# The first output tile of five large matrix products runs k-tile by k-tile beside other TensorE work, and the last square no longer passes through GpSimd

## The reference, cut to what matters

```
for li in range(2):
    g = norm_g[li]
    xn = rmsnorm(h, g[0])
    mix = mix_even(xn) if li == 0 else mix_odd(xn)       # RWKV-7 + mLSTM, or retention
    h = h + rmsnorm(mix, g[1])
    f = square(relu(rmsnorm(h, g[2]) @ ffn_up[li])) @ ffn_down[li]
    h = h + rmsnorm(f, g[3])
    h = h + sigmoid(h @ ple_gate[li]) * (p[li] @ ple_proj[li])
```

## Time and profile before

| | |
|---|---|
| median of 3 runs | 2152.05 us (2147.31 to 2153.11) |
| the profiled execution | 2154.12 us, of which the span of instructions is 2152.3 us |
| granted TensorE clock, mean | 0.942 |
| PE busy | 92% of the span |
| DVE / ACT / POOL busy | 46% / 31% / 3% |

### The profile page before, as it was taken

How to read it: one execution, slowest core, us unless ns; L and a number is a source line. 1 busy time by engine, 2 the same in 40 slices (tenths; PEclk the granted TensorE clock), 3 DMA queues, 4 the chain that set the end, 5 groups by cost and what they waited for, 6 DMA issues and landing times.

```text
span 2152.3 us, 39908 instructions
## 1 busy us (share of the span) xinstructions
PE 1975.4 (92%) x16899; PEld 1805.8 (84%) x16899; DVE 998.9 (46%) x1493; ACT 672.8 (31%) x928; POOL 72.3 (3%) x82
## 2 busy tenths in 40 slices
PE   8988887888587999999899999999999799999989
PEld 7967775777265999999899976666999699999978
DVE  6546762555514442342266745555642643234244
ACT  4222214323113332332243123335432433233222
POOL 0000000111000000000100000000001000000000
PEclk9998985889678999999999999999999899999999
DMA  5202110000221222222313224444223122222221
GB/s 197 96 30 79 40 64 0 3 2 3 101 81 48 78 89 97 88 88 97 108 49 118 88 90 177 179 171 186 99 90 96 40 97 88 89 97 88 89 97 60
DMA packets 44750, 187.01 MB, mean 87 GB/s; under 512 B 5480, under 2 KB 5992, under 8 KB 39272
## 3 DMA queue, kind: packets, MB, share of 16 engines
q1 hardware_dynamic: 44648, 185.53, 25.1%
HBM read 160.48 MB, written 25.03 MB: 86 GB/s over the span
## 4 chain that ended last, share of the span: by engine, by line
PE 84%; DVE 10%; ACT 3%; issue 2%; POOL 0%; DMA 0%; DVEq 0%; POOLq 0%; SPq 0%; ACTq 0%
PE ps L2136 52%; PE ps L2019 7%; PE ps L332 3%; PE ps L727 2%; PE ps L1681 2%; PE ps L2084 1%; DVE h_a L1909 1%; PE ps L2094 1%; PE ps L2078 1%; DVE free L414 1%; PE ps L1705 1%; PE ps L350 1%; PE ps L1667 1%; PE ps L2074 1%; DVE rb L369 1%
## 5 line engine op out<-in xcount | busy, mean ns | idle before, releaser
L2124 DVE TENSOR_TENSOR w_low<-slot,w_high 128x1024 fp32r<-128x1024 f32 x240 | 293.5, 1224 | 495.0 <-ACT w_high L2120 494.9
L2120 ACT ACTIVATE w_high<-slot 128x1024 fp32r<-128x1024 f32 x240 | 254.0, 1059 | 797.6 <-PE ps L2136 709.5
L2136 PE MATMUL ps<-x_high,w_high 128*128 128x260 f32 x1600 | 323.3, 283 | 1.1 <-issue 1.1
L2136 PE MATMUL ps<-x_high,w_low 128*128 128x260 f32 x1600 | 322.9, 283 | 0.0
L2136 PE MATMUL ps<-x_low,w_high 128*128 128x260 f32 x1600 | 322.4, 283 | 0.0
L2136 PE MATMUL ps<-hidden_high,w_low 128*128 128x260 f32 x1536 | 309.5, 283 | 0.0
L2136 PE MATMUL ps<-hidden_high,w_high 128*128 128x260 f32 x1536 | 309.4, 283 | 0.0
L2136 PE MATMUL ps<-hidden_low,w_high 128*128 128x260 f32 x1536 | 309.0, 283 | 0.0
L2136 PEld LDWEIGHTS ps<-x_high,w_high 128*128 128x128 f32 x1600 | 247.7, 189 | 1.8 <-issue 1.5
L2136 PEld LDWEIGHTS ps<-x_high,w_low 128*128 128x128 f32 x1600 | 247.2, 189 | 0.0
L2136 PEld LDWEIGHTS ps<-x_low,w_high 128*128 128x128 f32 x1600 | 246.6, 189 | 0.0
(11 more groups left out here) (555 smaller groups left out, 2634.4 us busy)
## 6 DMA issues: line engine op xcount, KB each, us to landing
slot<-in_w SPq DMA_DIRECT2D x240, 512.0 KB, 3.8
h_a<-in_rst SPq DMA_DIRECT2D x16, 1024.0 KB, 4.9
out_rst_o<-h_a SPq DMA_DIRECT2D x16, 1024.0 KB, 3.9
slot<-in_w SPq DMA_DIRECT2D x2, 2048.0 KB, 8.4
h_a<-in_x SPq DMA_DIRECT2D x4, 520.0 KB, 5.2
h_a<-in_x SPq DMA_DIRECT2D x1, 2080.0 KB, 7.6
out_y<-h_a SPq DMA_DIRECT2D x8, 260.0 KB
con<-in_con SPq DMA_DIRECT2D x1, 2062.0 KB, 16.0
```

Source lines behind the costliest of these rows:

```text
L2120: nc.scalar.activation(wh[c % 2], raw[c % 4], ACT.Copy).then_inc(s_wh, 1)
L2124: nc.vector.tensor_tensor(wl[c % 2], raw[c % 4], wh[c % 2].bitcast(F32), ALU.subtract).then_inc(s_wl, 1)
L2136: mm = pe.matmul(ps[:, 2 * par + hf, 0:HALF], w[c % 2][:, at], y(kt, hf), start=(start and kt == 0 and w is wh and y is x), stop=(stop and ...
```

## The change

1. `pe_prenorm` takes a function `beside`. After the norm product of k-tile kt it runs the 6 matmuls of k-tile kt-1 of the next product's first output tile (`first_tile`), and the last one after the loop. The first of them waits for the PSUM pair, for `w_low` of chunk 0, and each for its `x_low`. This is done at `in0`, `up0a` and `up1a`.
2. At the start, ACT makes `w_high` of chunk 0 ahead of k-tile 5, and DVE makes its `w_low` behind `x_low` 5; chunk 1 stays last.
3. In `pe_proj` the gate's first tile goes in beside the embedding products: k-tiles 0 to 3 behind products 4 to 7, then k-tiles 4 to 7. ACT copies products 0 and 1 out before its first `hh` copy, and from there product mt+2 behind `hh` mt.
4. `pe_postnorm` multiplies twice: `ss`, now the sum of only 7 squares, and then the eighth square itself (`sqr[1]`), added in PSUM. POOL makes one addition fewer per norm.
5. The loops over output tiles begin with the second group of four; tiles 1 to 3 stand in front of the loop as code of their own.

```diff
-        def pe_prenorm(pe, n):
+        def pe_prenorm(pe, n, beside=None):
             for kt in range(KD):
                 pe.wait_ge(s_xg, 8 * n + kt + 1)
                 for hf in range(2):
                     mm = pe.matmul(ps[:, 4 + hf, 0:HALF], C("mean_d"),
                                    hid[:, 24 + kt, hf * HALF:(hf + 1) * HALF], start=(kt == 0), stop=(kt == KD - 1))
-            mm.then_inc(s_st, 1)
+                if kt == KD - 1:
+                    mm.then_inc(s_st, 1)
+                if beside and kt:
+                    beside(kt - 1)
+            if beside:
+                beside(KD - 1)
 
         def pe_postnorm(pe, n):
-            pe.wait_ge(s_ss, 8 * n + 8)
-            for hf in range(2):
-                mm = pe.matmul(ps[:, 4 + hf, 0:HALF], C("mean_d"), ss[:, hf * HALF:(hf + 1) * HALF],
-                               start=True, stop=True)
+            for first, sums, w in [(True, ss, (s_ss, 7 * n + 7)), (False, sqr[1], (s_sq, 8 * n + 8))]:
+                pe.wait_ge(*w)
+                for hf in range(2):
+                    mm = pe.matmul(ps[:, 4 + hf, 0:HALF], C("mean_d"), sums[:, hf * HALF:(hf + 1) * HALF],
+                                   start=first, stop=not first)
             mm.then_inc(s_st, 1)
...
-        def act_prenorm(act, n, h, gain, ready, xg):
+        def act_prenorm(act, n, h, gain, ready, xg, ahead=None):
             for kt in range(KD):
+                if kt == 5 and ahead:
+                    ahead()
                 act.wait_ge(*ready(kt))
...
         def pool_sum(pool, n):
-            for mt in range(KD):
+            for mt in range(KD - 1):
                 pool.wait_ge(s_sq, 8 * n + mt + 1)
...
+        def first_tile(pe, t0, base, waits, x=part_of(xh), lo=part_of(xl)):
+
+            def beside(kt):
+                if kt == 0:
+                    pe.wait_ge(s_bank, t0 + 1)
+                    pe.wait_ge(s_wl, base + 1)
+                for w in waits(kt):
+                    pe.wait_ge(*w)
+                mm = pe_step(pe, 0, 0, x, lo, kt, True, True)
+                if kt == KD - 1:
+                    mm.then_inc(s_tile, 1)
+            return beside
...
+            gate_tile = first_tile(pe, GEMMS[f"gate{lyr}"][1], CHUNKS[f"gate{lyr}"],
+                                   lambda kt: [(s_gl, 8 * lyr + kt + 1)], part_of(hh, 8), part_of(hl))
             for mt in range(KD):
                 if mt >= 2:
                     pe.wait_ge(s_pjc, 8 * lyr + mt - 1)
...
                 mm.then_inc(s_pj, 1)
+                if mt >= 4:
+                    gate_tile(mt - 4)
+            for kt in range(4, KD):
+                gate_tile(kt)
 
         def act_ple(act, lyr, hn, more):
             a = nc.scalar
-            for mt in range(KD):
-                act.wait_ge(s_h, 8 * (2 * lyr + 1) + mt + 1)
-                a.activation(hh[:, 8 + mt, :], hb[lyr][:, mt, :], ACT.Copy).then_inc(s_gh, 1)
-                act.wait_ge(s_pj, 8 * lyr + mt + 1)
-                p4 = 4 + 2 * (mt % 2)
-                a.activation(two(hid[:, mt, :]), ps[:, p4:p4 + 2, 0:HALF], ACT.Copy).then_inc(s_pjc, 1)
+            for mt in range(-2, KD):
+                if mt >= 0:
+                    act.wait_ge(s_h, 8 * (2 * lyr + 1) + mt + 1)
+                    a.activation(hh[:, 8 + mt, :], hb[lyr][:, mt, :], ACT.Copy).then_inc(s_gh, 1)
+                if mt + 2 < KD:
+                    act.wait_ge(s_pj, 8 * lyr + mt + 3)
+                    p4 = 4 + 2 * (mt % 2)
+                    a.activation(two(hid[:, mt + 2, :]), ps[:, p4:p4 + 2, 0:HALF], ACT.Copy).then_inc(s_pjc, 1)
...
             pe.wait_ge(s_first, 32)
-            pe_prenorm(pe, 0)
-            pe_split(pe, "in0", lambda kt: [(s_xl, kt + 1)], only=NB)
+            pe_prenorm(pe, 0, first_tile(pe, GEMMS["in0"][1], CHUNKS["in0"], lambda kt: [(s_xl, kt + 1)]))
+            pe_split(pe, "in0", None, only=NB, begun=True)
...
-            act_prenorm(act, 0, hb[0], 0, lambda kt: (s_x[kt // 2], 16), xh)
-            for c in range(2):
-                act_high(act, 0, c)
+            act_prenorm(act, 0, hb[0], 0, lambda kt: (s_x[kt // 2], 16), xh, lambda: act_high(act, 0, 0))
+            act_high(act, 0, 1)
...
             for kt in range(KD):
                 dve.wait_ge(s_xg, kt + 1)
                 dve_x_low(dve, hb[0], 0, kt)
-            for c in range(2):
-                dve_low(dve, 0, c)
+                if kt == 5:
+                    dve_low(dve, 0, 0)
+            dve_low(dve, 0, 1)
```

More of the change, by code:

```diff
@@ L2124, in dve_low, with pe_step @@
             nc.vector.tensor_tensor(wl[c % 2], raw[c % 4], wh[c % 2].bitcast(F32), ALU.subtract).then_inc(s_wl, 1)
+        part_of = lambda t, k0=0: (lambda kt, hf: t[:, k0 + kt, hf * HALF:(hf + 1) * HALF])
+        def pe_step(pe, c, par, x, lo, kt, start, stop):
+            at = slice(kt * P, (kt + 1) * P)
+            for w, y in [(wh, x), (wh, lo), (wl, x)]:
+                for hf in range(2):
+                    mm = pe.matmul(ps[:, 2 * par + hf, 0:HALF], w[c % 2][:, at], y(kt, hf),
+                                   start=(start and kt == 0 and w is wh and y is x),
+                                   stop=(stop and kt == 7 and w is wl))
+            return mm
         def pe_chunk(pe, base, c, i, par, x, lo, start, stop, waits=None):
@@ L2132, in pe_chunk, with pe_split @@
                         pe.wait_ge(*w)
[L2133 to L2138, removed]
-            return mm
-        part_of = lambda t, k0=0: (lambda kt, hf: t[:, k0 + kt, hf * HALF:(hf + 1) * HALF])
-        def pe_split(pe, name, waits, hi=part_of(xh), lo=part_of(xl), only=None):
+                mm = pe_step(pe, c, par, x, lo, kt, start, stop)
+            return mm
+        def first_tile(pe, t0, base, waits, x=part_of(xh), lo=part_of(xl)):
[9 more added lines that the diff above has]
+            return beside
+        def pe_split(pe, name, waits, hi=part_of(xh), lo=part_of(xl), only=None, begun=False):
             t0, n = GEMMS[name][1], only or GEMMS[name][3]
@@ L2149, in tile @@
                 pe_chunk(pe, CHUNKS[name], m, i, m % 2, hi, lo, True, True, waits).then_inc(s_tile, 1)
-            with pe.Fori(0, n // 4) as i:
+            if begun:
+                for m in range(1, 4):
+                    tile(m)
+            with pe.Fori(int(begun), n // 4) as i:
                 for m in range(4):
@@ L2170, in pe_ffn, with up_tile @@
                 t0 = GEMMS[up][1]
-                with pe.Fori(0, HH // 4) as i:
-                    for m in range(4):
[L2173 to L2176, removed]
-                        pe_chunk(pe, FFN_CHUNKS[lyr], 32 * part + m, i, m % 2, part_of(xh), part_of(xl), True, True,
-                                 waits).then_inc(s_tile, 1)
+                def up_tile(m, i=0):
+                    pe.wait_ge(s_bank, (t0 + m + 1) + 4 * i)
+                    pe_chunk(pe, FFN_CHUNKS[lyr], 32 * part + m, i, m % 2, part_of(xh), part_of(xl), True,
+                             True).then_inc(s_tile, 1)
+                if part == 0:
+                    for m in range(1, 4):
+                        up_tile(m)
+                with pe.Fori(1 - part, HH // 4) as i:
+                    for m in range(4):
+                        up_tile(m, i)
                 t0 = GEMMS[down][1]
@@ L2456, in _ @@
             pe_postnorm(pe, 0)
-            pe_prenorm(pe, 1)
+            pe_prenorm(pe, 1, first_tile(pe, GEMMS["up0a"][1], FFN_CHUNKS[0],
+                                         lambda kt: [(s_xl, 8 + kt + 1)]))
             pe_ffn(pe, 0)
@@ L2466, in _ @@
             pe_postnorm(pe, 2)
-            pe_prenorm(pe, 3)
+            pe_prenorm(pe, 3, first_tile(pe, GEMMS["up1a"][1], FFN_CHUNKS[1],
+                                         lambda kt: [(s_xl, 24 + kt + 1)]))
             pe_ffn(pe, 1)
```

12 lines of the change are left out of this document (6 added, 6 removed).

## The result

The changed kernel takes 2144.02 us, median of 20 runs (2135.21 to 2152.11), against 2152.66 us for 20 runs of the kernel before. The two medians differ by 8.6 us. The ratio, which is estimated over all of the runs, is 0.9957, 95% interval 0.9943 to 0.9971: faster by 9.3 us, between 6.2 and 12.3. The profiled execution took 2148.49 us and its span 2146.7 us, 5.6 less than the one of before.

The account below looks back on a forecast made before the run. PE, busy 92% of 2152.3 us, was taken as the bound. Gains of 6.7 + 4.3 + 3.2 + 3.2 minus a loss of 8.6 gave 8.8 us less, 2152.05 to 2143.3 us; range 2138 to 2151.

Parts of the forecast that it names:

- Place 1: Start of in0: norm products queued behind the wait for w_low delay tile 2, a loss of 8.6 us.
- `in0` wins nothing back: Rest of in0: DVE evacuates 5.77 us apart, PE's own pace, so the start's loss is not recovered.
- Place 2: up0a: first tile interleaved with the norm products ends at 698.3 instead of tile 1 at 704.99, gain 6.7 us.
- The lower bound, 3.2: up0a: gain left if the clock still falls for a stretch of 7 us, 3.5 us less.
- Place 5: up1a: P7, T6, T7 end at 1707.7 against 1711.95, gain 4.3 us (0.8 with a clock drop).
- Places 3 and 6: The two gates: earlier postnorm and first tile beside the embedding products, gain 3.2 us each, bounds 1.5 and 4.5.
- the 1.1 named: First gate: DVE's `hl` 7 at most 1.1 us later, since ACT's `hh` copies stand behind copies waiting for PE.
- its upper bound of 4.5: Each gate: largest gain, 4.5 us, where DVE's `hl` 7 sets the end.
- Interleaving is free: PE: changing between fp32 norm products (0.88 us) and fp32r k-tiles (0.72 us) costs no extra time.
- the clock stays low wherever tile and products are interleaved: Rival for interleaved stretches with waits: half clock makes the kernel 12.1 us slower, 2164 us; chance 0.08.
- the start loses nothing: Rival at in0: DVE hides the norm products behind the wait, 17.4 us less, 2134.7 us; chance 0.06.
- the gains only just pay: Rival for the sum: gains only just cover the start's loss, 1.5 us less, 2150.5 us; chance 0.30.

Follow-up runs that it names:

- start_late: Changed kernel, but the first tile of in0 begins behind the norm product of k-tile 6 instead of 1; 2135.58 us, ratio 0.9901.
- start_only: Kernel before with only the start (in0) changed; 2160.33 us, ratio 1.0033.
- start_sooner: Changed kernel with w_high of chunk 0 ahead of k-tile 3 and its w_low behind k-tile 2; 2139.67 us, ratio 0.9926.
- start_filled: Changed kernel plus ten unused matmuls (20 records) between the second norm product and the first tile of in0; 2141.99 us, ratio 0.9936.
- before again: Kernel before with no edit, executed once more to see how stage lengths repeat; 2151.91 us.
- gates_only: Kernel before with only the gates' first tiles between the embedding products and ACT's new copy order; 2148.99 us, ratio 0.998.
- postnorm_only: Kernel before with only the last square multiplied by PE itself; 2151.49 us, ratio 0.9995.
- after_again: Changed kernel with no edit, executed once more (its second execution); 2142.81 us.

## Why the prediction was right

It said 2143.3 us, 8.8 less. Measured were 2144.02 us, 8.6 less by the medians and 9.3 by the ratio. Step by step:

- **Place 1, the loss of 8.6 us.** Right in its mechanism: PE idle 5.19 us (5.2), tile 0 at 16.99 (17.0), clock 0.50 behind it, tile 1 at 30.14 (30.4), and tile 2 waits for `w_low` 2. `start_late` shows that the queue behind the wait is the cause. Tile 2 comes 7.2 us later than before, not 8.6; two steps failed here. "Queued behind it are ACT's table load 1.28 and root 0.6": the load ran ahead of the wait, at 18.22, so 1.28 fall away. "`in0` wins nothing back" was right, but it also loses: from tile 2 to the end it takes 81.39 us and not 80.61. In all of the kernels in which the evacuation of tile 0 comes late (start_only, start_sooner, start_filled too) this stage is 81.37 to 81.39, elsewhere 80.61 to 80.67; in the kernel after, tile 3 is held by DVE's `w_low` (the row at 43.49). 7.2 + 0.8 = 8.0. The size is that of one execution: in the second the clock rose earlier, and it is 6.4 + 0.8 = 7.2.
- **Place 2, 6.7 us.** The first pair shows 6.65, but the term leaned on the clock's fall from 694 to 701 in the one execution shown. Every other kernel with the old order (before again, start_only, gates_only, postnorm_only) took 32.56 to 32.58 there, so the usual gain is 4.3 us, and the size was right for one execution only. The lower bound, 3.2, held. So the size of 6.7 that the first pair confirms is in part luck.
- **Place 5, 4.3 us.** Measured 21.45 against 17.15 in the two kernels. In `gates_only` and `postnorm_only` the old order took 23.03 and 22.87, since the clock fell later and was still low behind the last square, so it can be 5.8. The new order took 17.14 to 17.16 in each kernel that has it, and `up0a` 28.25 to 28.28.
- **Places 3 and 6, 3.2 us each.** Measured 2.98 and 3.36. The first gate had its four records at almost full clock (1.36 us) and its root 2.12 earlier (2.15 taken); the second had them at half clock (2.10 us) and its root 1.36 earlier, the near bound of 1.3, and won it back in the products, whose first five took 10.25 us there and 11.35 at the first gate. At the first gate DVE waited 1.37 us for `hidden_high` behind copies that wait for PE, against the 1.1 named. In the second execution the second gate gained 4.3, near its upper bound of 4.5.
- **Interleaving is free.** From 22.15 to 23.75 one norm product and one k-tile take 1.60 us, the 0.88 + 0.72 of the prices.
- **The rivals.** That the clock stays low wherever tile and products are interleaved fell: it is 1.00 from 698 to 711, and in the same part of `up0a` and `up1a` in all eight profiles with that order. The Trainium skill, "TensorE: Matmul & The Clock Gate", section "Loop structure matters more than you think", says that a long DMA wait between every matmul makes PE go cold. The trace agrees in that the one long wait of 5.19 us at the start had 0.50 behind it. The interleaved stretch is no case of this rule: its waits, one in front of each norm product, are short ones for ACT, 0.34 us in each 2.2, and the clock stayed at 1.00. That the start loses nothing fell with `start_only`. That the gains only just pay fell by the interval, whose weak end is 6.2 us, just short of the 6.5 that the prediction called the limit of a measurement.

So the sum came out right partly since errors offset, which is luck: the start lost 0.6 less (1.4 in the second execution), and place 2 usually gives 2.4 less, than the prediction had. By the stages' usual lengths it is 4.3 + 3.0 + 4.3 to 5.8 + 3.4 - 8.0, 7.0 to 8.5 us less; the measured 9.3 (6.2 to 12.3) cannot be told from that.

## What to carry to other kernels

Interleave a stalled chain with other work only where the operands of that work are really there: an in-order engine puts everything behind the first wait, and here the same edit that won 8.6 us in two places, by their usual lengths, cost 7 to 8 at the start, and one number (seven norm products ahead of the tile, not two) gave them back. When you sum places, check each place's length in a second execution of the same kernel before you trust a difference of a few microseconds, above all where the clock falls in a stretch that is only half busy. Look for the longest operation behind the work that you delay (here the 3.40 us reciprocal in front of the first evacuation) and not at the engine's own total.

## What the runs showed of the hardware

- The same code, 5,297 matmul records between `in0` and `out0`, took 554.2 to 564.5 us, at a mean granted clock of 0.85 to 0.83. One and the same kernel went from 557.0 to 564.5.
- A stretch of 7 us in which PE was busy 3.5 to 3.8 us was followed by a clock of 0.51 in one execution (`before`, 694 to 701) and of 1.00 in another of the same kernel. In the old order the clock fell again in 6 of 10 such stretches. The interleaved stretch, busy 11.5 of 13 us with waits of 0.34 us, kept 1.00 in all 16.
- ACT's table load takes 1.28 us, and no further pause is seen: in `start_late` it starts at 18.41 and the root behind it at 19.71.
- An idle time of 5.19 us was followed by half clock for about 4.5 us, and one of 4.76 us in `after_again` for about 2.9 us (16.77 to 19.62). One of 1.32 us in `start_sooner` was followed by the full clock. Filling the 5.19 us with 20 records kept 1.00 and brought tile 1 1.7 us earlier than in the first execution of the changed kernel, 0.75 earlier than in the second.
- ACT's table load can run ahead of the wait of the instruction that needs it: here 9.41 us ahead of the root. At 39.20 us of the same kernel another load began only behind 7.32 us of idle time. What decides between the two was not tried.
